# Order of work at the beginnings of the stages in a two-block transformer kernel in fp32

## What is computed

```python
h = rmsnorm(x, g_mix)
c_q, c_kv, k_r, u_pool, z, xbc, dt, lru_g, lru_x, gates = split(h @ w_in)
y_a = mla_mixer(c_q, c_kv, k_r, ...)      # latent attention: rmsnorm(c_q) @ w_uq, rmsnorm(c_kv) @ w_ukv
y_b = pool_mixer(u_pool, w_pool, ...)     # four moving averages, each through a 128x128 matrix
y_c = ssd_mixer(z, xbc, dt, ...)
y_d = rglru_mixer(lru_g, lru_x, ...)
merged = sum(sigmoid(gates[b]) * (y[b] @ w_branch[b]) for b in range(4))
x = x + merged @ w_out
x = x + square(relu(rmsnorm(x, g_mlp) @ w_ff1)) @ w_ff2
x = x + (p @ w_ple) * sigmoid(rmsnorm(x, g_ple) @ w_ple_gate)
x = rmsnorm(x, g_final)                   # then the second block, which begins
                                          # with rmsnorm(x, norm1) * (1 + mod) + mod @ w_in_2
```

## Time and profile before

| | us |
|---|---|
| median of 3 runs | 3635.59 |
| lowest and highest | 3633.96, 3638.15 |
| the profiled execution | 3629.72 |
| its span | 3627.9 |
| PE busy | 3435.8 |
| DVE busy | 2273.3 |
| ACT busy | 1582.6 |
| POOL busy | 813.8 |

### The profile page before, as it was taken

How to read it: one execution, slowest core, us unless ns; L and a number is a source line. 1 busy time by engine, 2 the same in 40 slices (tenths; PEclk the granted TensorE clock), 3 DMA queues, 4 the chain that set the end, 5 groups by cost and what they waited for, 6 DMA issues and landing times. The chain is left out here.

```text
span 3627.9 us, 43936 instructions
## 1 busy us (share of the span) xinstructions
PE 3435.8 (95%) x17289; PEld 2810.7 (77%) x17289; DVE 2273.3 (63%) x2919; ACT 1582.6 (44%) x1968; POOL 813.8 (22%) x403
## 2 busy tenths in 40 slices
PE   7999999999989999999999889999788799999998
PEld 6666777677868778887887767777676799999997
DVE  3334445635447675665764754546755899999998
ACT  4344443334321343331213433342544677777776
POOL 3101111112212345544432211111222110111112
PEclk9999999999999999999999999999899899999999
DMA  5111113133455223335541223131632999999998
GB/s 196 48 40 59 54 64 112 64 111 125 151 200 179 95 86 114 112 138 189 206 174 52 85 89 136 65 117 69 209 118 92 371 384 386 385 381 380 380 380 314
DMA packets 131725, 626.75 MB, mean 173 GB/s; under 512 B 14849, under 2 KB 15241, under 8 KB 106690
## 3 DMA queue, kind: packets, MB, share of 16 engines
q1 hardware_dynamic: 126626, 606.12, 44.9%
q0 software_dynamic: 4752, 17.30, 1.7%
q10 hardware_dynamic: 144, 0.52, 0.0%
HBM read 520.67 MB, written 103.19 MB: 172 GB/s over the span
## 5 line engine op out<-in xcount | busy, mean ns | idle before, releaser
L264 PE MATMUL bank<-XH,WH 128*128 128x512 f32 (+1 forms) x2312 | 925.0, 400 | 44.2 <-ACT stg L2379 8.6
L266 PE MATMUL bank<-XH,WL 128*128 128x512 f32 (+1 forms) x2312 | 898.6, 389 | 0.0
L265 PE MATMUL bank<-XL,WH 128*128 128x512 f32 (+1 forms) x2312 | 896.2, 388 | 0.0
L252 POOL TENSOR_TENSOR WL<-WR,WH 128x1024 fp32r<-128x1024 f32 (+1 forms) x177 | 407.1, 2300 | 1777.4 <-ACT WH L244 1777.4
L264 PEld LDWEIGHTS bank<-XH,WH 128*128 128x128 f32 x2312 | 437.5, 189 | 165.6 <-issue 39.2
L265 PEld LDWEIGHTS bank<-XL,WH 128*128 128x128 f32 x2312 | 437.9, 189 | 94.4 <-issue 6.5
L266 PEld LDWEIGHTS bank<-XH,WL 128*128 128x128 f32 x2312 | 437.5, 189 | 91.4
L244 ACT ACTIVATE WH<-WR 128x1024 fp32r<-128x1024 f32 (+1 forms) x177 | 173.3, 979 | 544.5 <-PE bank L266 530.4
L3594 DVE TENSOR_TENSOR EL<-ER,EH 128x2816 fp32r<-128x2816 f32 x120 | 371.4, 3101 | 4.5 <-POOL warm L3884 4.5
L3589 ACT ACTIVATE EH<-ER 128x2816 fp32r<-128x2816 f32 x120 | 307.5, 2564 | 114.9 <-PE bank L3659 83.5
L3657 PE MATMUL bank<-EH,WH 128*128 128x352 f32 x1024 | 335.4, 328 | 1.5 <-DVE WL L3781 1.5
(11 more groups left out here) (620 smaller groups left out, 5864.1 us busy)
## 6 DMA issues: line engine op xcount, KB each, us to landing
ER<-in_wu_dram SPq DMA_DIRECT2D x48, 1408.0 KB, 8.9
ER<-in_wd_dram SPq DMA_DIRECT2D x40, 1408.0 KB, 11.1
WR<-in_w_in_dram SPq DMA_DIRECT2D x89, 512.0 KB, 4.4
ER<-in_wg_dram SPq DMA_DIRECT2D x32, 1408.0 KB, 8.9
WR<-in_w_ff_dram SPq DMA_DIRECT2D x64, 512.0 KB, 4.7
aq<-in_w_ada_dram SPq DMA_DIRECT2D x48, 512.0 KB, 3.5
res<-in_wg_dram SPq DMA_DIRECT2D x16, 1408.0 KB, 8.7
res<-in_wu_dram SPq DMA_DIRECT2D x16, 1408.0 KB, 8.5
```

Source lines behind the costliest of these rows:

```text
L252: e.tensor_tensor(WL[:, n % 2 * 1024:n % 2 * 1024 + m], raw, hi.bitcast(F32), ALU.subtract).then_inc(*w_lo.up("w_lo", n))
L264: e.matmul(bank[bk][:, 0:b - a], whi, xhi, start=k == 0, stop=False)
L265: e.matmul(bank[bk][:, 0:b - a], whi, xlo, start=False, stop=False)
L266: mm = e.matmul(bank[bk][:, 0:b - a], wlo, xhi, start=False, stop=k == K - 1)
```

## The change

Nothing is computed otherwise. Instructions stand at other places, and two pairs of buffers are used for the last squares.

```diff
@@ attention_pe @@
-        st.fill(24, "mla", "ang")
+        st.fill(14, "mla", "ang")
+        st.fill(10, "mla", "q squares")
         for s, key in enumerate(("q", "kv")):
             e.wait_ge(*on("mla.sum", s))
             rstd_pe(e, tA, T, (2, 3), ("mla", s))
-            st.fill(12, "mla", key)
+            if s == 0:
+                st.fill(8, "mla", key)
+                st.fill(9, "mla", "kv squares")
+            else:
+                st.fill(12, "mla", key)
@@ pool_sp, pool_pe @@
+            if g == 1:
+                branch_first_sp(e)
-            st.fill(24 if g == 0 else 16, "pool", g)
+            st.fill((20, 8, 9, 10)[g], "pool", g)
@@ branch_first_sp @@
         y_ready(e, 0)
+        y_ready(e, 3)
@@ branch_act @@
+            if 26 <= n < 30:
+                for h in range(2):
+                    wo_hi(e, h, n - 26)
         for h in range(2):
-            for j in range(8):
...
-                e.wait_ge(*on("w_used", 91))
...
+            for j in range(4, 8):
+                wo_hi(e, h, j)
@@ branch_dve @@
+            if n in (27, 29):
+                for h in range(2):
+                    wo_lo(e, V, h, n - 27)
         for h in range(2):
-            for j in range(8):
-                low(h, j)
+            for j in range(4, 8):
+                wo_lo(e, V, h, j)
...
                 if m == 7 and h == 1:
+                    factor_lo(e, T4, 0)
                     up_sum(e, 0, 3)
                     up_sum(e, 0, 4)
+                    up_sum(e, 0, 5)
+                    for i in (T3, T2, T4):
+                        factor_sum(e, i, 2)
+                    factor_lo(e, T4, 1)
+                    factor_lo(e, T2, 2)
                     factor_lo(e, T3, 2)
-                    factor_lo(e, T2, 2)
                     for i in (T3, T2, T4):
                         factor_sum(e, i, 3)
+                    factor_lo(e, T4, 2)
+                    factor_lo(e, T2, 3)
                     factor_lo(e, T3, 3)
-                    factor_lo(e, T2, 3)
@@ branch_pool @@
         for n in range(32):
+            if n == 31:
+                e.wait_ge(*on("wo.lo", 0, 7))
             w_split_lo(e, 62 + n)
+            if n in (28, 30):
+                for h in range(2):
+                    wo_lo(e, br_pool, h, n - 27)
@@ first_factors_act @@
         factor_b12(e, 2)
+        factor_hi(e, T4, 0)
+        factor_hi(e, T4, 1)
+        up_hi(e, 0, 3)
+        up_hi(e, 0, 4)
+        factor_hi(e, T2, 2)
         factor_hi(e, T3, 2)
-        factor_hi(e, T2, 2)
+        factor_hi(e, T4, 2)
         factor_b12(e, 3)
@@ first_factors_dve: the three factor_sum(..., 2) are taken out @@
@@ ff_pe_ @@
-                if n == 0 and i == 3:
+                if n == 0 and i == 4:
                     e.wait_ge(*on("wo.sum"))
                     rstd_pe(e, acq, T, (4, 0), ("ff",))
@@ ff_act_, and ff_pool_ alike with the low parts @@
+            if t == 0:
+                w_split_hi(e, N_FF + 2)
             for j in down_at(t):
                 down_hi(e, j)
-            w_split_hi(e, N_FF + t + 2)
+            if t:
+                w_split_hi(e, N_FF + t + 2)
@@ ple_act: the last tile's squares go to buffers of their own, its weight split behind them @@
+        for h in range(2):
+            e.wait_ge(*on("ple.res", 7, h))
+            for k, g in enumerate((1.0, pr("g_final", 7))):
...
+                e.activation(last_square(h, k), xc(7)[:, half(h)], AF.Square, scale=g).then_inc(*A.up("ple.sq", 14 + h, k))
+        w_split_hi(e, N_PLE + 9)
@@ ple_dve: the last tile's first half is finished before the second half's product is awaited @@
@@ fin_pe: sum and second sum of a half behind each other, each as soon as its own addition is done @@
-        e.wait_ge(*on("ple.sum"))
-        rstd_pe(e, acq, T, (6, 7), ("fin",))
         for h in range(2):
+            e.wait_ge(*on("ple.add", 14 + h, 0))
...
+            e.wait_ge(*on("ple.add", 14 + h, 1))
             e.wait_ge(*on.bank(4 + h, "fin.msq", h))
@@ fin_act: the logarithms of a half behind each other; fin_dve: waits for the sum, no longer for the logarithm @@
```

More of the change, by code:

```diff
@@ L2240, in ff_pool_ @@
     def ff_pool_(e):
-        for i in (2, 3, 4, 6, 5):
+        for i in (2, 3, 4, 5, 6):
             up_lo(e, 0, i)
@@ L2296, in squares @@
                         *A.up("ple.sq", i, 1))
-        for m in range(8):
+        for m in range(7):
             for h in range(2):
@@ L2303, in ple_act, with last_square @@
             squares(m)
+        for h in range(2):
+            e.wait_ge(*on("ple.ev", 7, h))
+            e.activation(q_slot(h), q_slot(h), AF.Tanh, scale=0.5).then_inc(*A.up("ple.tanh", 7, h))
+        for h in range(2):
+            e.wait_ge(*on("ple.res", 7, h))
+            for k, g in enumerate((1.0, pr("g_final", 7))):
+                if h == 0:
+                    e.wait_ge(*on("ple.add", 13, k))
+                e.activation(last_square(h, k), xc(7)[:, half(h)], AF.Square, scale=g).then_inc(*A.up("ple.sq", 14 + h, k))
+        w_split_hi(e, N_PLE + 9)
+    def last_square(h, k):
+        return rN[:, half(k)] if h else zs[:, half(k)]
     def ple_dve(e):
@@ L2310, in add @@
                     e.wait_ge(*on("ple.sq", i, k))
-                    e.tensor_tensor(a[:, half(i % 2)], a[:, half(i % 2)], zs[:, half(k)], ALU.add).then_inc(
-                        *V.up("ple.add", i, k))
-        for m in range(8):
+                    sq_ = last_square(i % 2, k) if i >= 14 else zs[:, half(k)]
+                    e.tensor_tensor(a[:, half(i % 2)], a[:, half(i % 2)], sq_, ALU.add).then_inc(*V.up("ple.add", i, k))
+        for m in range(7):
             for h in range(2):
@@ L2330, in ple_dve @@
                 add(2 * m + h - 1)
+        for h in range(2):
+            q, rs = q_slot(h), xc(7)[:, half(h)]
+            e.wait_ge(*on("gemm", N_PLE + 7, h * 512))
+            e.wait_ge(*on("ple.res", 6, h))
+            e.tensor_tensor(q, bank[(14 + h) % 6][:, :], rN[:, half(h)], ALU.mult).then_inc(*V.up("ple.ev", 7, h))
+            if h == 0:
+                add(13)
+            e.wait_ge(*on("ple.tanh", 7, h))
+            e.wait_ge(*on("ple.pw", 7))
+            e.scalar_tensor_tensor(q, q, 1.0, pw[:, 7 * T + h * 512:7 * T + h * 512 + 512], ALU.add, ALU.mult).then_inc(
+                *V.up())
+            e.wait_ge(*V.now)
+            e.scalar_tensor_tensor(rs, q, 0.5, rs, ALU.mult, ALU.add).then_inc(*V.up("ple.res", 7, h))
+        add(14)
         add(15)
-        on.at["ple.sum",] = V.now
     def ple_pool(e):
@@ L2428, in fin_pe @@
     def fin_pe(e, st):
-        e.wait_ge(*on("ple.sum"))
-        rstd_pe(e, acq, T, (6, 7), ("fin",))
         for h in range(2):
+            e.wait_ge(*on("ple.add", 14 + h, 0))
+            e.wait_ge(*on.bank(6 + h, "fin", "mean", h))
+            e.matmul(bank[6 + h][:, :], ones, acq[:, half(h)], start=True, stop=True).then_inc(*pe_norm.up("fin", "sum", h))
+            e.wait_ge(*on("ple.add", 14 + h, 1))
             e.wait_ge(*on.bank(4 + h, "fin.msq", h))
             e.matmul(bank[4 + h][:, :], ones, ac2[:, half(h)], start=True, stop=True).then_inc(*f_pe.up("fin.sum2", h))
-            on.bank(6 + h, "fin.msq", h)
         st.until(2, "fin")
@@ L2455, in fin_act @@
                 *act_norm.up("fin", "mean", h))
-        for h in range(2):
             e.wait_ge(*on("fin.msq", h))
```

54 lines of the change are left out of this document (23 added, 31 removed).

## The result

The changed kernel took 3597.81 us (median of 4 runs, 3595.33 to 3602.02), the kernel before 3635.51: a ratio of 0.9899 with a 95% interval of 0.9887 to 0.9911, 37.7 us less. The forecast was 33.4 less. The profiled execution has a span of 3593.5 us against 3627.9, 34.4 less, at a mean granted clock of 0.982 against 0.978.

What follows compares the result with a forecast made beforehand. TensorE, busy 3435.8 of 3627.9 us, was taken as the bound, so only its waits and slow-clock stretches count. Seven terms summed to 33.4 us less, from 3635.6 to 3602; range 3590 to 3619.

Steps and rivals of the forecast that it cites:

- 1. Two norms: Attention's two norms: old waits go, a new 7.6 us wait for bank 1 comes; -0.6 us, bounds -2.1 and +0.9.
- 2. Mixers: All mixers: filling units end five steps earlier, removing a 2.36 us wait; +1.5 us, bounds -1 and +2.5.
- 3. Pool and first branch: Pool stage to first branch: earlier loads and eleven filling steps behind the pool leave 3.7 us; gain +7.0, bounds 5.5 and 8.
- 4. `w_out`: Branches to `w_out`: four of eight pieces ready early, so 0.5 us of 7.1 remains; gain +6.6, bounds 5 and 7.1.
- 5. Feed-forward: `w_out` to feed-forward: banks freed earlier, a new 3.4 us wait in the fourth unit; gain +3.5, bounds 0.8 and 6.2.
- 6. Tile 102: Second product's third tile: earlier weight split removes a 5.21 us wait and 2.7 of slow clock; +7.9, bounds 6.9 and 7.9.
- 7. Final norm: Final norm before the second block: first half finished earlier, so sums start sooner; gain +7.5 us, between 8.2 and 5.1.
- (a): Rival: new waits, such as unit 15's and the fourth unit's, take half the gain back; 3618 us, chance 0.11.
- (b): Rival: at places 3, 4, 6 and 7 another operand is equally late, leaving 4.4 us gain; 3631 us, chance 0.04.
- (c): Rival: SP's queue stands at the pool stage behind late fourth-mixer stores, ending slower; 3647 us at 80 late, chance 0.05.

Runs made afterwards that it cites:

- the second run: Changed kernel, but ACT splits tile 8 ahead of the first norm's logarithm, unit 13's copy staying behind the norm products: 3594.29 us, ratio 0.9892.
- The two runs of this place: Changed kernel with DVE's list and norm sums reordered at the feed-forward's start: 3597.84 us; the same plus ACT's two second-block weight splits ahead of the norm: 3596.31 us.
- the run with halves: Changed kernel, but the first branch's input is split in halves of 512 tokens, tile 61's weight behind the first four: 3594.71 us, ratio 0.9892.
- the first run: Changed kernel, but DVE copies unit 13 out of bank 1 ahead of the first norm's sums, as before: 3587.93 us, ratio 0.9877.

## Why the prediction was right, and where a step was off

**The bound** was read rightly: TensorE's busy time is nearly the same, and the gain sits at the places named, in all but the mixers with the rows named. That the sum came so near, 32.5 for 33.4, is in part luck: 2.6 too little at the mixers stands against 1.0, 1.4 and 1.4 too much at places 1, 3 and 7, and the mixers' figure is that of one execution.

**1. Two norms: -0.6 forecast, -1.6 measured.** The mechanism held: no wait for `PT` at the first norm, and one for bank 1 right behind its sums. 7.6 was worked out, and 7.55 is what it is without POOL's overlap (the second run); with it 9.64. The step that was mis-sized is the overlap, put at 0.8 though its own pair of rows showed 2.16: it costs 2.1. The lower bound of this place, by its own terms (7.6, 2.7 and 2.2 against 10.1), is -2.4 and not -2.1. The Trainium skill, SBUF — State Buffer, section SBUF: two separate sides, has this as an exclusive lock for a whole instruction; by that rule the prediction worked out -2.0, the nearer figure, and the pair of rows in the second run agrees with it (5.76 and 3.68). What the prediction did not ask is whether the copy had to stand there at all.

**2. Mixers: +1.5 forecast, +4.1 measured**, outside its bounds of -1 to +2.5. The reason given failed: the 2.36 us wait for ACT's copy, at the start of the 85th unit, is replaced by one of 1.72 at that of the 82nd (771.99), 1.7 to 3.0 us in the other profiles with this filling. The gain is 2.4 in the rglru stage, where POOL's weight splits leave DVE's rows, and 2.1 in attention, where 0.9 of it is of this kind. The prediction counted units and copies, and not where the moved splits fall on DVE; and its list of waits left out fourteen in the mixers of 0.16 to 1.14 us, 9.3 together. The size is less certain than the table makes it look: with the ssd stage at 56.2 to 59.7 us, the three stretches together gained 0.5 to 4.1 from profile to profile.

**3. Pool and first branch: +7.0 forecast, +5.6 measured.** What was to be left before the first product, 3.7, is 3.73. Two other terms were too small. The wait for the last average was put at nothing, and 0.79 of its 1.88 is left. DVE and POOL show why:

```profile
998.20 1.16 DVE L1495 TENSOR_TENSOR ptmp<-ptmp,con 128x16 f32<-128x16 f32 x1
997.75 1.58 POOL L252 TENSOR_TENSOR WL<-WR,WH 128x512 fp32r<-128x512 f32 x1 [11.87 <-ACT WH L244]
```

The same row takes 0.18 us in the other three groups, so by these rows nothing would be left without the overlap. And the slow steps cost more: the first 16 take 13.64 us, 2.6 over the full rhythm, where they took 12.72 and 1.7 over before, so 0.9 is lost where 0.5 had been put. The whole first unit ran at the lower level, 5.25 us (1014.03 to 1019.28) against 2.75 at the full one. That the loads belonged to the cause was wrong; the filling alone does it.

**4. `w_out`: +6.6 forecast, +7.2 measured.** No wait at all is left where 0.5 was allowed. The slow clock's share is not a fixed price: with the split put back the same wait cost 6.1 in all, where the prediction had read 7.1. In the `w_out` stage itself 1.6 us were lost again; see below.

**5. Feed-forward: +3.5 forecast, +3.5 measured**, and by its steps: the wait in the fourth unit is 3.83 (3.4), that for bank 0 behind the sums 0.78 (0.8), the slow clock behind it within 0 to 2.7 (six matmuls in 2.72 us instead of 1.37, so 1.4, where the sum had 1.3). That it agrees to the tenth is luck: the wait is 0.4 longer, and 1 had been set aside for unseen order. The two runs of this place add that removing such a wait need not pay: the norm behind it bounds the place.

**6. Tile 102: +7.9 forecast, +7.6 measured**, 8.1 at the tile itself and 8.5 alone in the kernel before. ACT's split of tile 102 now follows directly on the last product of tile 100, 14 us ahead of its use at 1626.68:

```profile
1612.30 1.06 ACT L244 ACTIVATE WH<-WR 128x1024 fp32r<-128x1024 f32 x1 [3.11 <-PE bank L266]
```

Tile 103 is next late, as said: POOL ends its low part at 1637.27 and TensorE takes it up at 1637.67.

**7. Final norm: +7.5 forecast, +6.1 measured.** From the end of the last product of `ple` to the second block's first it is 16.0 us instead of the 15 named. The order held; the clock did not come back for the four sums, as the rows of the changed kernel show,

```profile
2053.18 1.91 PE L2488 MATMUL bank<-aq,con 128*128 128x512 f32 x2
2054.88 1.92 PE L2485 MATMUL bank<-aq,con 128*128 128x512 f32 x2
2056.59 1.34 PE L2488 MATMUL bank<-aq,con 128*128 128x512 f32 x2
```

while in the run with halves, with the same code and the same 3.51 us wait ahead, they were shorter:

```profile
2053.88 1.54 PE L2499 MATMUL bank<-aq,con 128*128 128x512 f32 x2
2055.26 1.02 PE L2496 MATMUL bank<-aq,con 128*128 128x512 f32 x2
2056.12 1.02 PE L2499 MATMUL bank<-aq,con 128*128 128x512 f32 x2
```

Over the profiles with this code the stretch took 14.5 to 16.2 us against 22.2 before, so the gain lies between 6.0 and 7.7.

**The rivals.** (a) New waits took nothing like half back: they came where forecast, 9.64 and 3.83 for 7.6 and 3.4, and no place that had none got one over 3 us. (b) Each edit did what it says, with the six loads as the exception, which did nothing. (c) SP did not stand: in the changed kernel it issued the six loads at 984.28, right behind the transfer before them.

## To carry to other kernels

Before moving filling work or a weight split, look at which rows of DVE the POOL half of that split will lie on: here that decided 2 us at the first norm, 2.4 in the rglru stage and about 1 each in attention, in the ssd stage (lost) and at the last pool product (lost), while the prediction looked at one wait of 2.36. Where two edits go after one wait, ask of each alone whether the other already covers it. And behind a removed wait look for the next dependency of the same place (here the norm), since a wait in its shadow is worth nothing.

## What the hardware showed that was not expected

**POOL against DVE, both ways and in small rows.** A DVE row of 128x128 took 1.95 us instead of 0.29, one of 128x16 1.16 instead of 0.18 and one of 128x1024 with one tensor input 2.72 instead of 0.81, each while POOL made a low part of 1.6 to 3.3 us. In the first run POOL suffered as well: two rows in 5.88 us, where one alone took 2.45 in the second.

**A slower rhythm at the full granted clock.** In the changed kernel's profile the matmuls from 1196 to 1282 start 0.233 us apart; in eleven of twelve other profiles it is 0.229 there. The row of the view by stretches, in whose columns the granted clock is the third from the end:

```profile
1196.00:1282.00 86.00, 86.00 (x370) 69.67 (x369) 51.75 (x62) 30.83 (x50) 19.90 (x9) 1.00 0.25 80
```

That is the 1.6 us lost in `w_out`. None of the other runs with the early splits has it over that stage, and the run with the splits put back has a part of it (85.65 us for the stretch, 84.5 to 84.7 in the others), so it does not belong to the change. Its cause stays open.

**The second block's own spread.** From its first product to the end the code is the same in all kernels. The view by stretches for the kernel before, the changed one and the one with `w_out`'s split back:

```profile
2095.37:3627.90 1532.53, 1427.27 (x8429) 1259.57 (x8429) 1136.31 (x1042) 861.05 (x807) 247.71 (x101) 0.97 0.66 251
2063.81:3593.50 1529.69, 1424.63 (x8429) 1256.75 (x8429) 1136.94 (x1042) 861.21 (x807) 248.73 (x101) 0.97 0.67 252
2068.18:3603.50 1535.32, 1431.53 (x8429) 1263.15 (x8429) 1135.77 (x1042) 861.06 (x807) 249.69 (x101) 0.96 0.66 251
```

Over all profiled executions it took 1529.6 to 1535.3 us, and TensorE's busy time moves with it. The 2.8 us that the changed kernel gained here lie within that spread, so no part of the change is credited with them.
